# Twelve products for the modulation, its weights in quarters, squares added by VectorE, and the last rows singly, in a two-block kernel

## The reference

```
first block
  h += 0.5 * swiglu(rms_norm(h))            feed-forward of width 2816, weights w1
  h += hybrid_mixer(rms_norm(h)) @ w_out    16 heads of attention in two kinds
  h += 0.5 * swiglu(rms_norm(h))            weights w2
second block
  ada = silu(c) @ ada_w + ada_b             c: 1024, ada_w: 1024 x 6144
  sh1, sc1, g1, sh2, sc2, g2 = split(ada, 6)
  u = rms_norm(h) * (1 + sc1) + sh1
  z = u @ w_in                              eight parts of 1024 columns
  y_a = (gated linear recurrence over zq, zf, zi) * silu(zg) @ w_a
  y_b = silu(layer_norm(conv31(zca * sigmoid(zcb)))) @ w_b
  h += g1 * ((sigmoid(zga)*y_a + sigmoid(zgb)*y_b) @ w_out)
  u2 = rms_norm(h) * (1 + sc2) + sh2
  h += g2 * peer(u2)    8 heads, each picks 16 of 16384 experts a token:
                        out = sum_k gate_k * gelu(u_tab[e_k] . u2) * v_tab[e_k]
  return rms_norm(h, final_g)
```

## Time and profile before

| | |
|---|---|
| median of three runs | 1566.13 us (1565.99 to 1567.95) |
| the profiled execution | 1569.3 us, its span 1567.3 us |
| mean granted TensorE clock | 0.978 |
| TensorE busy | 1457.9 us |
| VectorE busy | 1051.6 us |
| DMA | 571.91 MB, mean 365 GB/s |

### The profile page before, as it was taken

The page is one execution under the profiler, slowest core; times in us unless marked ns, Lnnn a source line. Parts: engine busy times, 40 slices in busy tenths (PEclk is TensorE's granted clock), DMA queues, the critical chain, the costliest instruction groups (busy, mean ns, idle before and its releaser), DMA issues.

```text
span 1567.3 us, 22748 instructions
## 1 busy us (share of the span) xinstructions
PE 1457.9 (93%) x8272; PEld 1120.1 (71%) x8272; DVE 1051.6 (67%) x2170; ACT 546.1 (35%) x1128; POOL 561.7 (36%) x382
## 2 busy tenths in 40 slices
PE   8999999999999999999999999998988978788777
PEld 7999998767999999998989995454444433333333
DVE  6655376876744328998975569775758585858556
ACT  5444354364544436443134252221212121212113
POOL 2455428220344441001002235444544444444441
PEclk9999999999999999999999999999999999989999
DMA  9888968997999998999976959999999999999996
GB/s 363 311 322 326 350 222 328 316 329 252 400 372 369 374 379 296 372 397 342 355 286 226 411 233 426 427 427 427 427 427 427 427 428 427 427 427 427 427 427 261
DMA packets 99814, 571.91 MB, mean 365 GB/s; under 512 B 11536, under 2 KB 11664, under 8 KB 50448
## 3 DMA queue, kind: packets, MB, share of 16 engines
q1 hardware_dynamic: 61056, 298.15, 51.6%
q0 software_dynamic: 37520, 268.47, 40.7%
q10 hardware_dynamic: 1152, 4.16, 0.7%
HBM read 569.67 MB, written 135.27 MB: 450 GB/s over the span
## 4 chain that ended last, share of the span: by engine, by line
PE 65%; DMA 25%; DVE 6%; issue 2%; POOL 2%; ACT 1%; ACTq 0%; DVEq 0%; POOLq 0%
DMA arena<-pairs,eidx 17%; PE ps L2727 9%; PE ps L2113 8%; PE ps L2112 8%; PE ps L2111 8%; DMA ring<-pairs,eidx 6%; PE ps L2504 5%; PE ps L2200 2%; PE ps L2198 2%; PE ps L2199 2%; PE ps L2453 2%; PE ps L2619 2%; PE ps L2520 2%; DVE arena L1965 1%; POOL w_lo L754 1%
## 5 line engine op out<-in xcount | busy, mean ns | idle before, releaser
L2727 PE MATMUL ps<-arena 128*128 128x512 f32 x844 | 398.2, 624 | 66.5 <-ACT arena L1252 66.5
L2727 PEld LDWEIGHTS ps<-arena 128*128 128x128 f32 x844 | 164.9, 199 | 284.8 <-issue 193.9
L1965 DVE CUSTOM_DVE_ANT_0 arena<-arena 128x1024 f32<-128x1024 f32 x211 | 255.0, 1223 | 148.3 <-DMA arena<-pairs,eidx 148.1
L822 POOL DMA_INDIRECT arena<-pairs,eidx x210 | 244.0, 1162 | 254.9 <-PE ps L2727 208.1
L754 POOL TENSOR_TENSOR w_lo<-ring,w_hi 128x1024 fp32r<-128x1024 f32 x76 | 208.0, 2739 | 259.6 <-DVE w_lo L1305 175.7
L2111 PE MATMUL ps<-u_hi,w_hi 128*128 128x256 f32 (+1 forms) x912 | 259.4, 284 | 1.8 <-POOL w_lo L754 1.6
L2113 PE MATMUL ps<-u_hi,w_lo 128*128 128x256 f32 (+1 forms) x912 | 259.5, 285 | 0.0
L2112 PE MATMUL ps<-u_lo,w_hi 128*128 128x256 f32 (+1 forms) x912 | 259.2, 284 | 0.0
L842 ACT ACTIVATE w_hi<-ring 128x1024 fp32r<-128x1024 f32 x188 | 197.8, 1056 | 149.9 <-PE ps L2200 71.2
L2111 PEld LDWEIGHTS ps<-u_hi,w_hi 128*128 128x128 f32 x912 | 172.1, 189 | 3.2 <-issue 2.3
L2113 PEld LDWEIGHTS ps<-u_hi,w_lo 128*128 128x128 f32 x912 | 172.3, 189 | 0.0
(11 more groups left out here) (394 smaller groups left out, 2507.4 us busy)
## 6 DMA issues: line engine op xcount, KB each, us to landing
ring<-in_stream SPq DMA_DIRECT2D x121, 1024.0 KB, 7.2
pairs<-in_peer_u SPq DMA_DIRECT2D x128, 512.0 KB, 7.6
pairs<-in_peer_v SPq DMA_DIRECT2D x128, 512.0 KB, 8.8
arena<-in_ada SPq DMA_DIRECT2D x32, 768.0 KB, 6.9
arena<-in_stream SPq DMA_DIRECT2D x8, 1024.0 KB, 10.3
arena<-pairs,eidx POOLq DMA_INDIRECT x210, 20.4
h<-in_x_t SPq DMA_DIRECT2D x2, 544.0 KB, 5.0
ring<-in_stream SPq DMA_DIRECT2D x2, 512.0 KB, 7.2
```

What stands on the lines that cost most here:

```text
L822: pool.indirect_dma_start(slot_of(n), None, pairs, own).then_inc(landing(n)[0], 16)
L1965: dve.tensor_tensor_reduce(row, row, hf[:, n % HEAD_ROWS // TOPK, :], 1.0, 0.0, ALU.mult, ALU.add, dots[:, n % HEAD_ROWS:n % HEAD_ROWS + 1 ...
L2727: mm = pe.matmul(ps[:, Y_BANKS[j // TOPK] + half, :], diag[:, n % DIAGS, :], slot_of(n)[:, D + half * 512:D + half * 512 + 512], start=(hd ...
```

## The change

1. The modulation's accumulator becomes 128 x 1536 instead of 128 x 4 x 1536: partitions 32g to 32g+31 hold quarter g of the columns. A load is four transfers of 32 rows each, onto 32 partitions each, so an add takes 32 rows of `ada_w` for all four quarters. `silu_c` becomes 128 x 32, filled by four small transfers of c. An add waits for the add before it. The sums are 12 products with a constant `quarter` (64 columns more of constants), all after the second feed-forward's first piece; none in the z stage. The bias and both gains are made once.
2. The eight last adds are spread over all eight tiles of `h` in the output projection; SyncE issues the second feed-forward's first piece behind the fifth of their loads, and its high and low parts come a tile or two sooner. TensorE's wait for the modulation moves from the third piece to the second half of the fourth.
3. In the z stage the shifts, bounds and the clearing move into the loop of low halves.
4. The first token tile's squares are added by VectorE, and one product makes the mean; the query's first half goes ahead of it, and the next tile is cut in two around the first scores.
5. The last sixteen rows go one by one; the steps of the first tile's norm move by a row or two.
6. In the last norm VectorE's half is one joined operation, and the halves change engines.

```diff
-SINGLE = ROWS - 3 * GROUP
+SINGLE = ROWS - 4 * GROUP
...
+    quarter = np.zeros((P, ADA_Q), np.float32)
+    quarter[np.arange(P), np.arange(P) // ADA_ROWS] = 1.0
...
             def load_ada(kt, q):
                 sp.wait_ge(ada_step, kt * ADA_Q + (q + 3))
-                n = kt * ADA_Q + q
-                sp.dma_start(ada_ring[:, q % 2, :], src).then_inc(ada_in[q % 2], 16)
+                for g in range(ADA_Q):
+                    n = kt * ADA_Q + g
+                    own = slice(g * ADA_ROWS, (g + 1) * ADA_ROWS)
+                    sp.dma_start(ada_ring[own, q % 2, :], src[q * ADA_ROWS:(q + 1) * ADA_ROWS, :]).then_inc(ada_in[q % 2], 16)
...
+            c_rows = a["cols"][:, COL["c"]:COL["c"] + KT].rearrange("(q r) k -> r q k", q=ADA_Q)
+            for g in range(ADA_Q):
+                sp.dma_start(own, c_rows).then_inc(c_in, 16)
...
-            with sp.Fori(0, KT // 2 - 2) as kt:
-                for q in range(ADA_Q):
-                    load_ada(kt + (KT // 2 + 2), q)
+            for n in range(2 * ADA_Q):
+                load_ada(KT - 2 + n // ADA_Q, n % ADA_Q)
+                if n == ADA_Q:
+                    load(BASE["ffn2"], BASE["ffn2"] % RING)
+            pair_up(at)
+            load_pieces(BASE["ffn2"] + 1, BASE["z_gate"], at + 1, 1)
...
-                    if n == 2 and k == 4:
+                    if n == 2 and k == 2:
                         piece = BASE["ffn2"]
...
-                dve.wait_ge(ada_step, kt * ADA_Q + (q + 1))
-                dve.scalar_tensor_tensor(ada_acc[:, q, :], ada_ring[:, q % 2, :], silu_c[:, bass.ds(kt, 1)],
-                                         ada_acc[:, q, :], ALU.mult, ALU.add).then_inc(ada_step, 1)
+                dve.wait_ge(ada_step, kt * ADA_Q + (q + ADA_Q))
+                dve.scalar_tensor_tensor(ada_flat, ada_ring[:, q % 2, :], silu_c[:, bass.ds(q * KT + kt, 1)],
+                                         ada_flat, ALU.mult, ALU.add).then_inc(ada_step, 1)
...
+            ADDS_BEFORE = {0: (0, 1), 1: (2,), 2: (3,), 3: (4,), 4: (5,), 5: (6,), 7: (7,)}
...
-                if m == 5:
+                if m == 4:
                     low(1, BASE["ffn2"], BASE["ffn2"] % RING)
...
-            dve.wait_ge(ada_mm, 2)
...
             for n in range(2 * (BASE["z_gate"] - BASE["z"] - 2)):
                 if n >= 2:
                     z_low(n)
+                if n == 3:
+                    then(dve.memset(pad_glu[:, :, 0:PAD], 0.0), lb_step)
+                if n in (4, 6):
+                    shifted((n - 4) * 2, (n - 4) * 2 + 4)
+                if n == 8:
+                    bounds()
...
+            def square_added(m):
+                first = slice(0, P)
+                dve.wait_ge(sq_done, 4 * KT + m + 1)
+                if m > 1:
+                    dve.wait_ge(tiles_added, 2 + m - 1)
+                dve.tensor_tensor(u[:, 0, first], u[:, 0, first], u[:, m, first], ALU.add).then_inc(tiles_added, 1)
...
-                    if n == ROWS - 11:
+                    if n == ROWS - 12:
                         gained(0)
...
-                    if n == ROWS - 9:
+                    if n == ROWS - 8:
                         squared(0)
-                    if n == ROWS - 6:
+                    if n == ROWS - 5:
                         scaled(0)
...
-            for half in range(2):
-                c = slice(half * HALF_D, (half + 1) * HALF_D)
-                then(dve.tensor_tensor(hf[:, 1, c], acc[:, 1, c], final_g[:, c], ALU.mult), fin_step)
+            then(dve.tensor_tensor(hf[:, 1, 0:HALF_D], acc[:, 1, 0:HALF_D], final_g[:, 0:HALF_D], ALU.mult), fin_step)
...
-            dve.tensor_scalar(acc[:, 1, 0:HALF_D], hf[:, 1, 0:HALF_D], fin[:, 9:10], None, ALU.mult).then_inc(half_out, 1)
+            dve.scalar_tensor_tensor(acc[:, 1, HALF_D:D], acc[:, 1, HALF_D:D], fin[:, 9:10], final_g[:, HALF_D:D], ALU.mult, ALU.mult
+                                     ).then_inc(half_out, 1)
...
-            def ada_sums(first, end):
+            def ada_sums():
                 pe.wait_ge(ada_step, KT * ADA_Q + ADA_Q)
-                for m in range(first, end):
-                    mm = pe.matmul(ps[:, 1, m:m + WIDE], flat[:, m * P:(m + 1) * P], C("ones")[:, 0:WIDE], start=True, stop=True)
+                for j in range(ADA_W // P):
+                    mm = pe.matmul(ps[:, 1, ADA_Q * j:ADA_Q * j + WIDE], ada_flat[:, j * P:(j + 1) * P], C("quarter"), start=True, stop=True)
...
-            tile_mean(0, 0, KT)
             pe.wait_ge(first_heads_in, 16 * FIRST_HEADS)
             first_query(0, 0)
+            first_mean()
             first_query(0, 1)
-            out_tile(1, 0)
+            out_tile(1, 0, 0, KT // 2)
             first_scores(0)
+            out_tile(1, 0, KT // 2, KT)
```

More of the change, by code:

```diff
@@ L258, in program @@
         place(0)
-        ada_acc = view(ADA_Q, ADA_W)
+        ada_acc = view(ADA_Q, ADA_W // ADA_Q)
+        ada_flat = ada_acc.rearrange("p q w -> p (q w)")
+        place(ADA_Q * ADA_W)
         ada_ring = view(2, ADA_W)
@@ L697, in _ @@
             at += BEFORE_ADA
-            with sp.Fori(0, KT // 2 - 2) as kt:
-                for q in range(ADA_Q):
-                    load_ada(kt + (KT // 2 + 2), q)
[L701 to L704, removed]
+            for n in range(2 * ADA_Q):
[4 more added lines that the diff above has]
+            load_pieces(BASE["ffn2"] + 1, BASE["z_gate"], at + 1, 1)
+            at += BASE["z_gate"] - BASE["ffn2"]
+            for part, end, each in (("z_gate", "w_b", 2), ("w_b", "w_out_2", 1)):
                 load_pieces(BASE[part], BASE[end], at, each)
@@ L1596, in _, with shifted, bounds @@
                 dve.tensor_tensor(z_tiles[:, tile, :], ps[:, bank, 0:SEQ], rstd[:, 0:SEQ], ALU.mult).then_inc(z_scaled, 1)
[L1597 to L1607, removed]
-            dve.tensor_scalar(lb[:, 1], lb[:, 0], -1.0, 1.0, ALU.mult, ALU.add).then_inc(lb_done, 1)
-            then(dve.memset(pad_glu[:, :, 0:PAD], 0.0), lb_step)
+            def shifted(first, end):
+                for k in range(first, end):
+                    dve.tensor_scalar(u[:, k, 0:SEQ], u[:, k, 0:SEQ], ada[:, k:k + 1], None, ALU.add).then_inc(u_done, 1)
+            def bounds():
+                dve.wait_ge(lb_e, 2)
+                then(dve.tensor_tensor(lb[:, 3], lb[:, 1], lb[:, 2], ALU.add), lb_step)
+                then(dve.reciprocal(lb[:, 4], lb[:, 3]), lb_step)
+                then(dve.tensor_tensor(lb[:, 0], lb[:, 1], lb[:, 4], ALU.mult), lb_step)
+                dve.tensor_scalar(lb[:, 1], lb[:, 0], -1.0, 1.0, ALU.mult, ALU.add).then_inc(lb_done, 1)
             cv = z[:, 0]
@@ L2160, in up @@
                     first = isinstance(piece, int) and piece == base + FFN_RAW[k]
-                    if k and first:
-                        pe.wait_ge(ada_done, 1)
                     if k and isinstance(piece, int) and piece == base:
@@ L2165, in up @@
                     for e in range(2):
+                        if k and e and isinstance(piece, int) and piece == base + 3:
+                            assert 2 * slot + e == 1, "the modulation's sums lie in this bank"
+                            pe.wait_ge(ada_done, 1)
                         ready = None
@@ L2605, in _, with out_tile @@
             last_product("w_a", KT, (o_hi, o_lo), o_lo_done)
-            def out_tile(t, m):
+            def out_tile(t, m, first=0, end=KT):
                 n = t * KT + m
@@ L2614, in out_tile @@
                 c = slice(t * P, (t + 1) * P)
-                for b in range(KT):
+                for b in range(first, end):
                     if n == 0:
@@ L2620, in out_tile, with first_mean @@
                                    start=(b == 0), stop=(b == KT - 1))
-                mm.then_inc(out_mm, 1)
+                if end == KT:
+                    mm.then_inc(out_mm, 1)
+            def first_mean():
+                pe.wait_ge(tiles_added, 2 + KT - 1)
+                pe.matmul(ps[:, STAT_BANKS[4], 0:P], C("mean_d"), u[:, 0, 0:P], start=True, stop=True).then_inc(ss_done, 1)
             def tile_mean(t, first, end):
```

70 lines of the change are left out of this document (40 added, 30 removed).

## The result

The changed kernel takes 1596.06 us (median of 4 runs, 1591.42 to 1605.87) against 1567.04 (4 runs, 1565.99 to 1568.54): a ratio of 1.0187, 95% interval 1.0161 to 1.0214, so some 29 us **slower**. I had forecast 1559.8, some 6 us the other way. The profiled execution took 1597.9 us with a span of 1596.1.

A forecast was written before the change was run, and what follows sets the result against it. The gather, DMA-bound at 426 GB/s, was taken as fixed, with TensorE's work ahead of it setting its start. Terms: -2.65 - 2.5 - 1.6 - 0.3 - 0.37 + 0.9 + 0.15 = -6.4; 1566.13 - 6.4 = 1559.8 us; 8 in 10 within 1557.0 to 1563.9.

The forecast's parts named there:

- The loads of the modulation's weights: Quartered weight loads onto 32 partitions each, in projection and output projection: 0.9 us lost, between 0 and 3.3.
- the upper end: Weight loads: the four transfers go one behind the other at half rate, 3.7 us instead of 1.84.
- my rival of the starving ring: First feed-forward: up to 3.9 us per load nothing happens; at 4.6 us, 11 us lost, 1571 us; chance 0.04.
- (a): First projection: at the loads' upper end the last add comes some 2.7 us later, stalling TensorE 1.3 us.
- (b): Output projection: second feed-forward's second piece loads behind the last adds' loads; norm 3.4 us later, 2.0 us lost.
- The rule of the Trainium skill that I cited: Weight loads: 32-partition transfers reach half the ports, different halves serialize; as rival, 3.3 us lost, 1562.1 us, chance 0.25.
- Sums once: Second feed-forward: modulation products run as 12 once, 2.65 us instead of 5.30; whole 2.65 us gained.
- z stage: z stage: the modulation's products there, 5.3 us, go; 2.5 us gained after stalls, between 1.0 and 5.3.
- First tile's squares: First token tile's squares ahead of the first query: 1.6 us gained, between 1.2 and 2.4.
- Last norm: Last norm: one joined VectorE operation lets the reciprocal start at the root's end; 0.37 us gained.
- Last rows: Last gathered rows taken singly: 0.3 us gained, at most 1.1 gained or 1.3 lost.

The follow-up runs named there:

- 1 quarters: Original kernel with each modulation-weight load as four transfers onto 32 neighbouring partitions each: 1596.74 us, ratio 1.0187.
- 3 halves: Original kernel with each modulation-weight load as two transfers onto 64 neighbouring partitions each: 1598.57 us, ratio 1.0213.
- 5 order: Changed kernel with the four quarters of a load issued in the order 0, 2, 1, 3: 1581.98 us, ratio 1.0102.
- 4 spread: Changed kernel with each quarter laid on every fourth partition, still four transfers a load: 1563.40 us, ratio 0.9975.
- 11 sums moved: Changed kernel, spread layout, one transfer a load, with the first feed-forward's last two sums one piece sooner each: 1559.95 us, ratio 0.9942.
- 10: Changed kernel, spread layout, one transfer a load, second feed-forward's second piece issued ahead of the last two modulation loads: 1561.55 us, ratio 0.9951.
- 12: Changed kernel, spread layout, one transfer a load, with both the sums moved sooner and the second piece issued sooner: 1561.88 us, ratio 0.9957.
- 7: Changed kernel with spread layout and one transfer a load, its source having 32 entries outermost: 1564.38 us, ratio 0.9978.

## Why the prediction was wrong

The table has TensorE's start at some places of the trace of before, and how much later (+) or sooner (-) each is in the others.

| place | before | after | 1 quarters | 3 halves | 5 order | 4 spread | 11 sums moved |
|---|---|---|---|---|---|---|---|
| ffn1, last down piece | 209.1 | +4.0 | -0.7 | -0.6 | -0.2 | -0.7 | -0.3 |
| projection, first squares | 237.7 | +20.8 | +14.5 | +12.6 | +7.6 | +0.6 | -1.0 |
| product behind the latents' norm | 288.1 | +32.9 | +27.6 | +28.4 | +17.1 | +1.3 | -1.1 |
| out-projection | 370.1 | +30.1 | +25.4 | +25.5 | +14.9 | +0.1 | -2.5 |
| its last product | 399.3 | +28.4 | +26.1 | +23.8 | +15.6 | -1.6 | -2.5 |
| z norm, last mean | 601.3 | +31.4 | +27.7 | +30.6 | +14.7 | -2.6 | -4.9 |
| z stage, last product | 717.0 | +29.8 | +27.6 | +30.5 | +12.2 | -5.1 | -6.6 |
| span | 1567.3 | +28.8 | +27.2 | +30.3 | +11.5 | -7.1 | -8.7 |

**The step that failed is "The loads of the modulation's weights"**: I put it at 0.9 us and at 3.3 at most, and experiment 1, which has this term alone, measures 29 us. It failed in three places.

*The price of a load.* I took 3.7 us as the upper end, and of what it leads to the lower half, because the landings of issues 0.33 us apart looked as if the four overlapped. The upper end was about right. At the 211 GB/s of 224 to 234 us a load of 768 KB takes 3.7 us. Its own packets (the rows of 6144 bytes as the DMA engines move them; mean duration in the traces from 43 to 200 us) say much the same. A load is 128 of them over 16 engines: at 238 ns each that is 1.9 us in before, at 383 ns 3.1 us in experiment 1, at 436 ns 3.5 us in after. The length of a turn (two pieces, one load, one block) has in it also what a load does to the transfers beside it. In after's timeline from the sum at 151.80 to that at 217.77 five turns take 65.97 us, 13.2 each. Before, a turn of 12.1 us had 0.89 of a queue that is full at 1.02: 12.1 x 0.89 / 1.02 = 10.6 us. So a load costs 2.6 us more than the 1.84 of its bytes, 4.5 us. VectorE's timeline in experiment 1 has the last two turns ahead of the evacuation in 25.14 us, 12.6 each:

```profile
185.66 1.82 DVE L1373 SCALAR_TENSOR_TENSOR arena<-arena,silu_c 128x1536 f32<-128x1536 f32 x1 [1.00 <-DMA arena<-in_ada]
...
210.80 3.40 DVE L1373 SCALAR_TENSOR_TENSOR arena<-arena,silu_c 128x1536 f32<-128x1536 f32 x1 [0.75 <-DMA arena<-in_ada]
```

By the same working that is 3.8 us a load, an estimate as the 4.5 is. It lies just under the 3.9 us up to which, by my rival, nothing happens, and the loss is 29 us all the same. So a larger price would not have saved the forecast. Why the turns of after are longer than those of experiment 1 stays open.

*What a full queue does.* This is the step that cost most. My rival of the starving ring counted only the ring's pieces, and these held: for nine turns nothing is late (9 x 1.1 us over the 12.1 of a turn are about the 11 us of slack that I had counted), and by the last TensorE has lost 4.0 us at most (nothing in experiments 1, 3 and 5). But the backlog that the ring's slack hides is in front of every other load too. The load issued at 208.28 landed 23 us later, and its sum stands on VectorE **ahead of the evacuation**: 14.0 us of TensorE. In experiment 1 the same sum waits 10.4 us and TensorE is 14.5 us late at the projection (table). I had asked who waits for the loads at two places, (a) and (b), and not at this one, where before the last two sums found their loads landed. A transfer that is in time in a queue with 12% to spare is the first to be late when there is none.

*The slack at (a) and (b).* At (a) I had the last sum 2.7 us later. But a load waits for the sum two before it, so there the sums keep the pace of the loads, and each load adds its own delay. VectorE's timeline before, then after:

```profile
244.09 3.22 DVE L1371 SCALAR_TENSOR_TENSOR arena<-arena,silu_c 128x1536 f32<-128x1536 f32 x1 [2.99 <-DMA arena<-in_ada]
```

```profile
266.97 3.59 DVE L1385 SCALAR_TENSOR_TENSOR arena<-arena,silu_c 128x1536 f32<-128x1536 f32 x1 [5.16 <-DMA arena<-in_ada]
```

From there to the last sum (270.44, and 304.46) five loads take 26.35 us before and 37.49 after: 2.2 us more each, 11 in all. The last sum is 34.0 us later, 13.2 more than TensorE was at the projection. TensorE's stall was priced 1.3 us: it is 10.7, and 2.7 more because TensorE, back from that wait, runs at a lower clock (+30.2 us where the 32 products of L2328 begin, +32.9 behind them). The window of that stretch in after has it granted 0.80 in the mean, a mixture of the levels of 1.2 and 2.4 GHz:

```profile
296.00:330.00 34.00, 23.27 (x171) 17.71 (x170) 19.85 (x29) 11.97 (x28) 6.52 (x6) 0.80 1.03 315
```

(b) had the place right and the size too small: out-projection's end to z norm goes from +28.4 to +31.4 us although the sums give 2.5 there, so 5.5 us are lost and not 2.0. The chain of after in that stretch (start, us, what) leads from a piece's load over ScalarE's splits to the norm's low parts:

```profile
429.64 12.12 DMA ring<-in_stream
441.78 2.01 ACT w_hi L855 x2
...
446.09 2.49 DVE u_lo L1356
```

It is the *third* piece's load, the next behind the second that I had named; both stand behind the last sums' loads in SyncE's order. In the spread kernel (4) the same load goes out at 396.29.

**The rule of the Trainium skill that I cited** (page "SBUF — State Buffer", section "Door 1: The DMA port swizzle") was right here: 32 neighbours at about half the rate, 64 no better (experiments 1 and 3). It says as well which partitions share a port, and by that every fourth partition reaches all of them; experiment 4, back at a share of 0.88, agrees. That transfers onto different halves serialize stands on the same page of the Trainium skill in the section "Can I just issue two DMAs to hit both halves?". Experiment 5 has it so for the most part (packets of 397 ns for 436), and yet 14 us went; that a queue which is only just full needs little to be in time again would explain it, and isn't shown. I gave the rule 0.25, and a time of 1562.1 that followed from the wrong account of who waits: the chance was low and the consequence lower. The same page of the Trainium skill, section "SBUF: two separate sides", has it that of a VectorE operation with two inputs in SBUF and a GpSimd operation that reads SBUF the one that starts first keeps their shared port for the whole instruction; the rows of 10 to 12 agree.

**The other steps** are read from the spread kernel and, where it doesn't matter, from after.
- *Sums once.* 12 products take 2.79 us in after, as counted. In experiments 7, 10 and 11 the stretch from the out-projection's end to the z norm gives 2.4 to 2.5 us of the 2.65; in 4 it gives 1.0, and the chain runs through the third piece's load there, so the rest goes to (b).
- *z stage.* 2.5 forecast; 1.6 in after, 2.5 in the spread kernel, 1.5 to 1.6 in 7, 10 and 11. Among TensorE's waits in after is the stall that I placed at the evacuated tile, 2.0 us for 2.1 (L1073 is ScalarE's evacuation in the z stage):

```profile
PE ps L2148 <- ACT arena L1073: 2.0, 1, 2.0
```

- *First tile's squares.* 1.6 forecast. The choice of experts is VectorE's at 941.05 where it was at 912.64: +28.4 us, against +29.9 at the start of the tiles ahead (TensorE's at 920.0 for 890.1). So 1.5 us. VectorE's timeline in after:

```profile
941.05 0.48 DVE L1857 MAX8 arena<-arena 128x8 f32<-128x128 f32 x2
```

- *Last norm.* From VectorE's first evacuation of the last half to ScalarE's last product before: 1563.75 - 1559.21 = 4.54 us. After, 1592.18 - 1587.94 = 4.24: 0.30 of 0.37. VectorE's timeline, then ScalarE's, in after:

```profile
1587.94 0.69 DVE L2117 TENSOR_TENSOR arena<-ps,arena 128x512 f32<-128x512 f32 x1 [1.79 <-PE ps L2767]
```

and

```profile
1592.18 0.72 ACT L1299 ACTIVATE arena<-arena 128x512 f32<-128x512 f32 x1 [0.30 <-DVE arena L2124]
```

- *Last rows.* With the norm 0.67 us forecast. From the first gather (917.35, and 945.76, 910.87, 909.33) to the end it is +0.4 in after, -0.6 in 4, -0.7 in 11. Too small to say more.
- *Not foreseen:* the lost race with GpSimd, +1.3 us ahead of the projection in 4 and 7; with the sums moved (11) the same stretch gives 0.7.

Without the load term my sum was -7.3 us. The spread kernel's trace has -7.1 in span, its timed ratio is 3.9 us (2.5 to 5.5). That the first comes so near is in part luck: the profiled execution of before lies 3.2 us above the median that I started from, and that of the spread kernel (1562.01 us) is the fastest of its ten. The ends of my range were added up wrongly too: all terms at their best ends make -11.7 and at their worst -0.5, not -10.9 and -0.9. The measured time lies far outside of either.

## What to carry to other kernels

Ask of every transfer which partitions it reaches, not only how many bytes it moves: the same 768 KB cost the queue some 1.9 us spread over the partitions and 3.1 to 4.5 on neighbouring ones, and a change of layout that was meant to save 5 us of TensorE turned a queue with 12% to spare into a full one. When a queue becomes full, its deep buffers hide that for a while; look for the youngest load that anything waits for, and for what stands behind that wait on its engine. And when one transfer is made of several blocks, look which dimension stands outermost.

## What the hardware showed that I had not expected

- One transfer with 4 entries outermost ran at 105 GB/s with three quarters of the DMA engines idle: 1719.86 us against 1564.38 with 32 entries outermost and the same bytes.
- Alternating lower and upper partitions took 14 us off the 29 us.
- Which of two operations 0.02 to 0.1 us apart starts first decides on which engine 1.5 or 2.2 us are lost: 3.91 in place of 2.40 on GpSimd, or 4.00 in place of 1.81 on VectorE.
